# Two projection chunks of a fused attention layer computed transposed: weights held, tokens streamed

## What is computed

```python
h = rms_norm(x, pre_norm_w[l])
proj = h @ w_in[l]
qa, za, ga, kc, vc, ksl, vsl, kw, vw, qb, kb, vb, zb = jnp.split(proj, splits, axis=-1)
...
def compress(k, pe, w1, w2):
    ...
    kc = k.reshape(b, hk, nchunk, CMP_STRIDE, dh)
    n_c = nchunk - r + 1
    blk = jnp.concatenate([kc[:, :, o:o + n_c] for o in range(r)], axis=3) + pe
    flat = blk.reshape(b, hk, n_c, CMP_LEN * dh)
    return jax.nn.gelu(flat @ w1) @ w2
```

## Time and profile before

| what | us |
|---|---|
| median of 3 runs (1828.54 to 1828.7) | 1828.62 |
| the profiled execution, its own time | 1828.58 |
| its span, first to last instruction | 1826.8 |
| PE busy (TensorE matmuls) | 1818.1 |
| PEld busy (TensorE weight loads, beside PE) | 1507.2 |
| DVE busy (VectorE) | 1062.3 |
| ACT busy (ScalarE) | 822.2 |
| POOL busy (GpSimd) | 192.1 |

### The profile page before, as it was taken

How to read it: one execution, slowest core, us unless ns; L and a number is a source line. 1 busy time by engine, 2 the same in 40 slices (tenths; PEclk the granted TensorE clock), 3 DMA queues, 4 the chain that set the end, 5 groups by cost and what they waited for, 6 DMA issues and landing times.

```text
span 1826.8 us, 23238 instructions
## 1 busy us (share of the span) xinstructions
PE 1818.1 (100%) x8402; PEld 1507.2 (83%) x8402; DVE 1062.3 (58%) x1100; ACT 822.2 (45%) x1062; POOL 192.1 (11%) x164
## 2 busy tenths in 40 slices
PE   9999999999999999999999999999999999999998
PEld 7888888888888888888888888888888888888886
DVE  7756656566665656644564456445644584445445
ACT  6644455454544444444444444444444454444442
POOL 2220002200102020022002200220022000000000
PEclk9999999999999999999999999999999999999999
DMA  9866687546455464666666656665666667776765
GB/s 296 248 194 185 190 238 224 167 128 185 137 173 162 139 173 132 187 189 186 171 186 191 188 163 193 186 191 165 186 193 186 176 186 216 211 212 203 213 208 194
DMA packets 183943, 344.77 MB, mean 189 GB/s; under 512 B 15152, under 2 KB 19376, under 8 KB 183856
## 3 DMA queue, kind: packets, MB, share of 16 engines
q1 hardware_dynamic: 183008, 342.45, 64.6%
q10 hardware_dynamic: 848, 1.07, 0.2%
HBM read 339.27 MB, written 4.19 MB: 188 GB/s over the span
## 4 chain that ended last, share of the span: by engine, by line
PE 98%; DVE 1%; DMA 0%; ACT 0%; issue 0%; DVEq 0%; ACTq 0%
PE acc L470 30%; PE acc L472 30%; PE acc L471 30%; PE trans L484 2%; PE heads L513 2%; PE scores L498 2%; PE acc L630 1%; DVE y L1348 0%; PE scores L619 0%; PE heads L551 0%; PE scores L531 0%; DMA norm_w<-in_norm 0%; PE trans L673 0%; DVE y L1342 0%; ACT w_parts L741 0%
## 5 line engine op out<-in xcount | busy, mean ns | idle before, releaser
L985 DVE TENSOR_TENSOR w_parts<-raw,w_parts 128x1024 fp32r<-128x1024 f32 x623 | 778.5, 1251 | 686.8 <-ACT w_parts L741 686.2
L741 ACT ACTIVATE w_parts<-raw 128x1024 fp32r<-128x1024 f32 x623 | 659.3, 1059 | 733.0 <-PE acc L472 724.4
L470 PE MATMUL acc<-w_parts,x_parts 128*128 128x512 f32 x2432 | 962.2, 396 | 1.0 <-DVE x_parts L1308 0.5
L472 PE MATMUL acc<-w_parts,x_parts 128*128 128x512 f32 x2432 | 948.3, 390 | 0.0
L471 PE MATMUL acc<-w_parts,x_parts 128*128 128x512 f32 x2432 | 946.9, 389 | 0.0
L472 PEld LDWEIGHTS acc<-w_parts,x_parts 128*128 128x128 f32 x2432 | 456.4, 188 | 97.0
L470 PEld LDWEIGHTS acc<-w_parts,x_parts 128*128 128x128 f32 x2432 | 456.8, 188 | 93.7 <-issue 2.0
L471 PEld LDWEIGHTS acc<-w_parts,x_parts 128*128 128x128 f32 x2432 | 457.1, 188 | 92.7 <-issue 1.0
L414 POOL TENSOR_TENSOR rot<-tok_a,trig 128x512 f32<-128x512 f32 x26 | 41.0, 1578 | 993.5 <-ACT tok_a L747 912.1
L753 ACT ACTIVATE probs_t<-trans 128x512 f32<-128x512 f32 (+1 forms) x40 | 23.1, 577 | 83.5 <-PE trans L484 77.8
L1256 DVE RECIPROCAL mixed<-mixed 128x256 f32<-128x256 f32 x32 | 55.9, 1747 | 0.5
(11 more groups left out here) (158 smaller groups left out, 579.4 us busy)
## 6 DMA issues: line engine op xcount, KB each, us to landing
raw<-in_w_in SPq DMA_DIRECT2D x479, 512.0 KB, 3.6
raw<-in_w_out SPq DMA_DIRECT2D x128, 512.0 KB, 4.3
raw<-in_w SPq DMA_DIRECT2D x16, 512.0 KB, 4.5
x_tok<-in_x SPq DMA_DIRECT2D x16, 256.0 KB, 5.0
xt_raw<-in_x_t SPq DMA_DIRECT2D x7, 512.0 KB, 5.7
out<-y SPq DMA_DIRECT2D x5, 512.0 KB, 3.0
wpost<-in_post_w SPq DMA_DIRECT2D x8, 256.0 KB, 5.0
gate_raw<-in_w_in SPq DMA_DIRECT2D x1, 768.0 KB, 8.2
```

The source lines that it names most:

```text
L470: nc.tensor.matmul(o, stat_hi, w_hi[:, s, kk, 0:width], start=(k == 0), stop=False)
L472: last = nc.tensor.matmul(o, stat_lo, w_hi[:, s, kk, 0:width], start=False, stop=(k == KB - 1))
L741: nc.scalar.activation(w_hi[:, n % SPLIT_SLOTS, :, 0:width], raw[:, n % RAW_SLOTS, :, 0:width], ACT.Copy).then_inc(hi_ready, 1)
L985: V.tensor_tensor(w_lo[:, s, :, 0:width], raw[:, n % RAW_SLOTS, :, 0:width], w_hi[:, s, :, 0:width].bitcast(F32), ALU.subtract).then_inc(l ...
```

## The change

KC and VC are computed the other way round. `gemm_pair_rows` holds a 128-column slice of the weights (one head) and streams the 256 tokens of `x_hi` or `x_lo`; a chunk then comes out with the head dimension on partitions and the tokens along the free axis, two heads to a bank. For each block and each of four heads there are three matmuls of 256 columns. The transposes of KC and VC, with the moves into and out of `trans`, are gone.

The inverse RMS is now needed along the free axis. VectorE writes it into `r_cols` (256 columns, each tile's value spread over 128 columns: the zeroed `hidden` plus `r[t]`), TensorE transposes it in two transposes before pair 2 of KC, and VectorE copies the result to `r_rows` after its sixth split of KC. `evacuate_rows` then multiplies each bank of 128 x 512 by `r_rows` straight into `k_t`, both banks on VectorE. ScalarE no longer moves out KC and VC.

```diff
-FILL_KSL, FILL_HIDDEN, FILL_GATE, FILL_KW, FILL_KC, FILL_VC, FILL_A = 4, 6, 7, (8, 10), 9, 11, 12
+FILL_KSL, FILL_HIDDEN, FILL_GATE, FILL_KW, FILL_KC, FILL_VC, FILL_A = 1, 3, 4, (5, 7), 6, 8, 9
...
+        r_cols, r_rows = gelu, hidden
...
+            def gemm_pair_rows(c, n, parity):
+
+                if n == 0:
+                    pe.wait_ge(acc0_free, c - 1)
+                    pe.wait_ge(acc1_free, c - 1)
+                pe.wait_ge(lo_ready, 16 * c + n + 1)
+                s = n % SPLIT_SLOTS
+                for kk in range(2):
+                    k = 2 * n + kk
+                    for h in range(HPG):
+                        o = acc[:, parity, h // 2, (h % 2) * SEQ:(h % 2 + 1) * SEQ]
+                        stat_hi, stat_lo = w_hi[:, s, kk, h * P:(h + 1) * P], w_lo[:, s, kk, h * P:(h + 1) * P]
+                        nc.tensor.matmul(o, stat_hi, x_hi[:, k, :], start=(k == 0 and h % 2 == 0), stop=False,
+                                         skip_group_check=True)
+                        nc.tensor.matmul(o, stat_hi, x_lo[:, k, :], start=False, stop=False, skip_group_check=True)
+                        last = nc.tensor.matmul(o, stat_lo, x_hi[:, k, :], start=False, stop=(k == KB - 1),
+                                                skip_group_check=True)
+                last.then_inc(weights_used, 1)
...
             for n in range(PAIRS):
-                gemm_pair(C_KC, n, 1)
-            for c, parity in ((C_VC, 0), (C_VW, 1)):
-                for n in range(PAIRS):
-                    if n in (1, 2):
-                        fill = 2 * (c - C_VC) + n - 1
-                        pe.wait_ge(acc0_free if n == 1 else acc1_free, c)
-                        transpose4(tok_a[:, n - 1, :], fill if fill else None)
-                    gemm_pair(c, n, parity)
+                if n == 2:
+                    pe.wait_ge(r_spread, 1)
+                    for t in range(TILES):
+                        last = nc.tensor.transpose(trans[:, t * P:(t + 1) * P], r_cols[:, t * P:(t + 1) * P], ident)
+                    last.then_inc(tr_done, 1)
+                gemm_pair_rows(C_KC, n, 1)
+            for n in range(PAIRS):
+                gemm_pair_rows(C_VC, n, 0)
+            for n in range(PAIRS):
+                gemm_pair(C_VW, n, 1)
...
-            evacuate(C_KC, 1, tok_a[:, 0, :], r0)
...
-            evacuate(C_VC, 0, tok_a[:, 0, :], r0)
...
                     dve.wait_ge(stats_ready, 1)
+                    for t in range(TILES):
+                        last = V.tensor_scalar(r_cols[:, t * P:(t + 1) * P], hidden[:, t * P:(t + 1) * P], r[t], None,
+                                               ALU.add)
+                    last.then_inc(r_spread, 1)
...
-                if at in (1, 2):
-                    take_fill(2 * i + at - 1, k_t[:, i, :, (at - 1) * P:at * P])
                 if at in (4, 5):
                     a = at - 4
-                    dve.wait_ge(tr_free, 2 * i + 2)
+                    dve.wait_ge(acc0_free, C_KC + i + 1)
+                    dve.wait_ge(acc1_free, C_KC + i + 1)
...
+            def evacuate_rows(c, parity, i):
+                dve.wait_ge(weights_used, PAIRS * (c + 1))
+                for j in range(2):
+                    V.tensor_tensor(k_t[:, i, 2 * j:2 * j + 2, :],
+                                    acc[:, parity, j, :].rearrange("p (h t) -> p h t", h=2),
+                                    r_rows[:, :].unsqueeze(1).broadcast_to([P, 2, SEQ]), ALU.mult
+                                    ).then_inc(acc0_free if j == 0 else acc1_free, 1)
+
             for n in range(LEAD, PAIRS + LEAD):
                 split(C_KC, n)
-            evacuate(C_KC, 1, tok_a[:, 1, :], r[1])
+                if n == LEAD + 2:
+                    dve.wait_ge(tr_done, 1)
+                    V.tensor_scalar(r_rows[:, :], trans[:, 0:SEQ], 1.0, None, ALU.mult).then_inc(tr_free, 1)
+                    dve.wait_ge(tr_free, 1)
+            evacuate_rows(C_KC, 1, 0)
             for n in range(LEAD, PAIRS + LEAD):
                 split(C_VC, n)
                 flat_rows(0, n - LEAD)
-            evacuate(C_VC, 0, tok_a[:, 1, :], r[1])
+            evacuate_rows(C_VC, 0, 1)
```

More of the change, by code:

```diff
@@ L213, in build @@
         masks_landed = sem("masks_landed")
+        r_spread = sem("r_spread")
         w2_landed = sem("w2_landed")
@@ L477, in gemm_pair @@
                     last.then_inc(last_tile0, 1)
+            def gemm_pair_rows(c, n, parity):
[15 more added lines that the diff above has]
+                last.then_inc(weights_used, 1)
             def transpose4(src, fill):
-                if fill is not None:
-                    pe.wait_ge(tr_free, fill)
+                pe.wait_ge(tr_free, fill)
                 for b in range(4):
```

## The result

The changed kernel takes 1832.38 us (median of 16 runs, 1832.11 to 1833.06) against 1828.67 for the kernel before (16 runs), +3.71 us; the ratio is 1.0021 with a 95% interval of 1.0014 to 1.0027. Forecast were +3.25 us and 1831.9. The profiled execution took 1832.3 us, its span is 1830.2. The measured change lies on the edge of the 0.2% that was named as what can be told from none, a hair above it (3.71 against 3.66).

A forecast was written before the change was run, and what follows sets the result against it. TensorE, busy through the whole span, was taken as the bound: 92.16 for 768 matmuls + 0.33 + 43.52 = 136.01 us against 132.76, +3.25, so 1828.62 became 1831.9 us. The range ran from 1825.7 to 1836.

The forecast's parts named there:

- The swap: KC and VC on TensorE: 192 matmuls of 512 columns each become 384 of 256, adding 5.1 us.
- d: Distance between starts of 256-column float32r matmuls with their loads in KC and VC, taken as 120.0 ns.
- case A: KC and VC matmuls: the 13.3 ns excess belongs to each instruction, 119 to 121 ns apart, +2.5 to +4.0 us; chance 0.50.
- Case B: KC and VC matmuls: excess per column or load floor, 112 to 113.3 ns apart, -2.9 to -1.9 us; chance 0.22.
- case E: KC and VC matmuls start 109 ns apart, like the transposes, -5.2 us, 1823.4; chance 0.04.
- The bound (b): TensorE: a 128 x 128 load takes about 112 ns, and no matmul start distance goes below that, except the transposes' 109.
- Case C: KC and VC: short matmuls never settle into the steady beat, 124.4 ns apart, +6.6 us, 1835.2; chance 0.20.
- Transposes: TensorE: four groups removed from VC and VW, -2.20 us; one group of two added in KC, +0.33 us.
- The other engines: ScalarE and VectorE work changes, VectorE about 1 us less; PE gets no new wait.
- All this costs zero: Changes off TensorE add nothing to the time, or 0.5 us if a cover proves thinner than read.
- the sum was added to the median: Whole kernel: profiled execution and median differ by 0.04 us, so 1828.62 + 3.25 = 1831.9.

The follow-up runs named there:

- e1: Kernel before, with every matmul of KC and VC cut into two of 256 columns, x still held and transposes kept: 1833.48 us.
- e7: Kernel before, with KC streamed 384 columns wide (fourth head left out) and every VC matmul cut into four of 128 columns: 1860.32 us.
- e5: Kernel before, with only 64 of the 128 tokens of each tile held in KC and VC: 1829.90 us.
- e4: Changed kernel, with x_hi and x_lo streamed together in one 512-column matmul under w_hi, x_hi alone under w_lo, a bank per head: 1830.33 us.
- e3: Kernel before without the four transpose groups of KC and VC; VectorE copies tok_a to k_t unturned, giving wrong data: 1826.39 us.
- e8: Changed kernel, with four instructions given back to ScalarE after the splits of KC and VC: 1832.02 us.
- e9: Kernel before, with ScalarE's two moves of KC and VC given to VectorE, shortening ScalarE's program: 1828.92 us.
- e10: e6 with the ScalarE fillers of e8: 1828.94 us, ratio to the kernel before 1.0001.
- e6: e4 with the matmuls of each pair of blocks grouped by width, eight of 512 columns, then eight of 256: 1829.29 us.

## Why the prediction was right

**The swap** is the term that decides, and it came as predicted: d = 120.0 ns against 120.0 taken, +5.1 us by the chunks (384 x 120.0 = 46.08 twice, against 43.52). The choice of case A rested on one inference, that the 13.3 ns above streaming belong to the instruction; e1, the changed kernel and e7 put three widths on one line: 120.0 at 256, 173.5 at 384, 226.7 at 512. The float32 rows that were given for it bear it out a little better than read: by the starts of the earlier trace rows four matmuls of 256 columns take 373.04 - 372.18 = 0.86 us, 215 ns each, 1.7 above streaming where the prediction had 0.7, against 2.3 at 512: twice the columns, and hardly more excess. The reason given with it, a start-up that half-rate float32 has time to hide, was tested by no run: the sum is confirmed, that reason is not. Case B (by columns, 113.3) is refuted by all of them, case E (109) with it. The gap formula of the Trainium skill (TensorE: Matmul & The Clock Gate, section Back-to-back issue gap), N/2.4 + 2.5 ns, which the page gives for an isolated matmul, is some 11 ns short at each width.

**The bound (b)**, 112 ns, held for float32r too (e7, 111 ns). At 256 columns there are 8 ns to spare, so the halving stopped just short of a second cost. That the bound is the load is argued, as said under e7.

**Case C** did not come, but its mechanism exists: 16.7 ns of excess in place of 13.3 where loads are shorter than 128 columns (e5) or widths alternate (e4). All 768 matmuls of the changed kernel have one width and full loads, and they settled: in VC every distance is 120 ns. Its price was put a little high (17.7), its place was wrong. Before the runs nothing told which sequences settle, so that this one did was not worked out but given a chance.

**Transposes.** Removed: -2.20 us predicted, -2.20 measured (e3). Added: 0.33 predicted, 0.21 measured (KC less VC). The 0.33 was 0.55 of a group of four less two steps of 109, and so carried over 0.11 us by which the wide matmuls behind such a group are late (0.55 - 4 x 0.109). Among narrow matmuls there is hardly any: two steps are 0.22 here, and in e1 a group of four costs (46.98 - 46.07) / 2 = 0.46 us.

**The other engines.** No wait was added on PE. The two `r_cols` writes took 0.48 us together (0.4 taken), and KSL's tile left at 94.33 + 0.74 = 95.07, 0.9 us ahead of KC:

```profile
92.80 0.48 DVE L1103 TENSOR_SCALAR gelu<-hidden,scl 128x128 f32<-128x128 f32 x2
93.20 1.22 DVE L1005 TENSOR_TENSOR w_parts<-raw,w_parts 128x1024 fp32r<-128x1024 f32 x1
94.33 0.74 DVE L1085 TENSOR_SCALAR tok_b<-acc,scl 128x512 f32<-128x512 f32 x1
...
104.39 0.41 DVE L1142 TENSOR_SCALAR hidden<-trans 128x256 f32<-128x256 f32 x1
...
142.47 1.29 DVE L1133 TENSOR_TENSOR k_t<-acc,hidden 128x512 f32<-128x512 f32 x2 [0.50 <-PE acc L496]
143.67 1.22 DVE L1005 TENSOR_TENSOR w_parts<-raw,w_parts 128x1024 fp32r<-128x1024 f32 x1
```

The two multiplies by `r_rows` took 1.29 us (1.4 taken), and the next split was done 2.6 us into VC (2.8 taken).

**Two steps failed** beside the ones that held, each by less than 0.4 us. The first is "All this costs zero", at the end of the prediction's paragraph on the other engines. ScalarE's lost moves were counted as time and not as program: four instructions less shifted a fetch into the output's writing, 0.37 us (e8, e9). The second is that the sum was added to the median as it stood, which takes what lies outside the span as unchanged; it grew from 1.78 to 2.1 us, and why is open. The account in profiled executions is then 3.01 (the last matmul: 3.16 for the chunks, 0.08 less by the earlier first matmul, 0.06 less in the stage before KC) + 0.37 (tail) + 0.35 (outside) = 3.7, as measured. The forecast of +3.25 came near 3.71 because its sum for TensorE was right within 0.1 us and the terms that it lacked are small. Without either of them the result would have stayed inside the 0.2%, to which +3.25 of 3.66 had been close already.

## What to carry to other kernels

Before turning a matmul around to save a transpose, look at how wide the streamed side becomes: count instructions, not columns alone. Here four groups of four transposes cost 2.2 us, and 384 more float32r instructions 5.1 us. Where two products share the held operand, streaming both moving operands in one instruction (e4) and keeping instructions of one width together (e6) won back 2.8 of the 5.1 us here. At this margin a version without transposes (e10) is level with one that has them, and no better. For differences under 1 us, take the time apart into the last matmul, the tail behind it, and what lies outside the span: here each of the last two moved by a third of a microsecond.

## What the runs showed of the hardware

- Float32r matmuls with full 128-column loads, back to back at the 2.4 GHz level (granted clock 1.00 in these stretches), come their columns plus 13.3 to 13.5 ns apart: 120.0, 173.5 and 226.7 ns for 256, 384 and 512, whichever operand is held (changed kernel and e1). Plain float32 at twice the cycles per column has an excess of about 2 ns (starts 215 and 429 ns apart). Why float32r pays more is open; half the load beside it does not make the excess smaller (e5: 230.0 ns).
- The excess is 16.7 ns in the mean where the load is of 64 columns (e5) or the width alternates (e4), in both with distances that repeat in a cycle of six matmuls. Within a run of equal ones it falls back to 13.3 after about five (e6). What the engine settles into was not found.
- Float32r of 128 columns keeps its rate; its starts are 111 ns apart (e7), which is more than streaming and excess, and most likely the load.
- A full PEld column is no sign of that bound: in the changed kernel loads of 192 ns start every 120 ns and show as busy all through, and 111 ns is possible (e7).
- A fetch of ScalarE's program that lands in the final output's writing goes with a tail that is 0.36 or 0.37 us longer, and four instructions more or less move it in or out (e8: 6.67 us against 7.03, e9: 7.03 against 6.66).
- The time can differ from the span by different amounts from kernel to kernel: 2.15 us in the mean for the changed kernel and e8, 1.77 to 1.80 for all others that ran more than once. The cause was not found.
